# RMS norms of a two-block transformer kernel: 1/rms as exp(-0.5 ln(ms + eps)) on ScalarE, one table set preloaded

## The chip, the cores and the metric

The kernel runs as one launch on one core of a Trainium2 chip. The metric is the device time of that launch in microseconds. A core has TensorE (matmuls, writing PSUM), VectorE, ScalarE and GpSimd, each with an instruction queue of its own that it works off in order, and SyncE, which issues the transfers here. The engines wait for each other through semaphores: an instruction in a queue that waits holds up all that stands behind it.

## What is computed

The reference is a model of three layers on 256 tokens of width 1024: a gated short convolution with a SwiGLU feed-forward, a sliding-window attention with a SwiGLU feed-forward, and a hybrid layer (attention and a gated linear recurrence side by side) with a squared-ReLU feed-forward. There are eight norms over the width, and one of each head of 64 for q and k in the first attention:

```python
def rmsnorm(x, gain):
    xf = x.astype(jnp.float32)
    r = lax.rsqrt(jnp.mean(xf * xf, axis=-1, keepdims=True) + EPS)
    return (xf * r).astype(x.dtype) * gain

x = x + short_conv_mixer(rmsnorm(x, norm_mixer[0]), ...)      # mix0
x = x + swiglu_ffn(rmsnorm(x, norm_ffn[0]), ...)              # ffn0
x = x + swa_sink_attention(rmsnorm(x, norm_mixer[1]), ...)    # mix1
x = x + swiglu_ffn(rmsnorm(x, norm_ffn[1]), ...)              # ffn1
u = rms_norm(h, attn_pre_norm)                                # pre2
mix = hybrid_mixer(u, ...)
h = h + rms_norm(mix, attn_post_norm)                         # post2
u = rms_norm(h, mlp_pre_norm)                                 # mpre
m = jnp.square(jax.nn.relu(u @ w_mlp_up)) @ w_mlp_down
h = h + rms_norm(m, mlp_post_norm)                            # mpost
```

## The kernel before

Everything is held with the width on the partitions: x is 8 tiles of 128 features by 256 tokens. All weights stream from memory once, in pieces of 8 blocks of 128x128. Each piece is split into two numbers of lower precision: ScalarE rounds it (`round_weights`, L743, tile `whi`), VectorE forms the rest (`rest_weights`, L1139, tile `wlo`), and TensorE multiplies (`blocks`, L397 to L403) with the activations, which are split likewise into the halves of `xa`, `xb` or `hid`. Four piece slots and four accumulators (PSUM banks 0 to 3) go round. Every engine's program is an order written out by hand; `next_weights(n)` in the queues of ScalarE and VectorE prepares the piece that TensorE needs four pieces later. TensorE may start a piece when its `wlo` is there (`lo_ready`) and when the accumulator has been emptied (`emptied`).

The norm is not applied to x before the matmul. The gain is put on x, the matmul runs on that, and 1/rms (`rbc`, a tile of 128x256 that has each token's value on all partitions) is multiplied onto the result. Meanwhile ScalarE squares the tiles (`square`, L764), GpSimd adds the squares (`add_square`, L1592 and L1595, tile `ssum`), and TensorE sums over the partitions (`stat`, L411). Then it goes one of two ways.

- Plain norms (ffn0, mix1, ffn1, pre2): one matmul with a square of ones (L418) gives the sum on all partitions, ScalarE takes the square root over 128x256 (`rms`, L774), VectorE the reciprocal (L1171).
- The norms in `TURNED` (mix0, post2, mpre, mpost): four narrow matmuls (L422, L426) put the tokens' sums on the partitions, 128x2. They take the last squared tile directly from `sq`, without GpSimd's addition. ScalarE takes the root of 128x2 (L774), VectorE the reciprocal of 128x2 (L1169), two matmuls with the identity spread it over 128x256 (`spread`, L438), and ScalarE copies that to `rbc` (`copy_spread`, L779).

Square root, Exp, Ln, Silu, Sigmoid and Gelu of ScalarE come from sets of tables. Where an instruction needs a function that is not in the loaded set, the build puts an ACT_TABLE_LOAD in front of it. Two small square roots (L783, L1084) exist only to bring that load forward.

The stages and where the norms stand in the queues:

- mix0, `bx` body: ScalarE's `bx_step` (i = 0, p = 0) does the spill copy, the root, the rounding of the next body's first piece, then the copy to `rbc`. TensorE's order is `AS_LOADED`.
- ffn0, mix1, ffn1, pre2: `first_body` in the order `STAIR`, with the norm's sum between the pieces.
- `o`, `wo`: projections whose results are added to x (`residual_part`), the squares of the next norm beside them. `gated_down` does the same for `dn0` and `dn1`; beside `dn0` a few small Exp and Ln (`decay_constant`, L815 and L818).
- attention (328 to 380 us): the norms of k and q (L909, L916, L1344, L1350), then for each pair of heads scores, mask, maximum, Exp, division, transposition, values.
- post2: after the last piece of `out2`, TensorE runs three matmuls that only keep it busy (`keep_warm`, L432), the sum, the spread and four more of them. ScalarE has, in this order: square of the last tile, `rms`, `next_weights`, `copy_spread`. VectorE has copy, reciprocal, `next_weights` and then the residual chain (`post_scaled` L1531, `post_add` L1537, `norm_lo` L1177), tile by tile, which feeds both the squares of mpre and `mup`.
- mpre: TensorE's order is `ONE_BY_ONE`; ScalarE's `squared_up` (i = 0, p = 0) has `rms`, spill copy, rounding of the next body's first piece, copy to `rbc`; VectorE has reciprocal, rest of that piece, sum of the first accumulator (L1154), ReLU and scale (L1560).
- mpost: the tail. Sum, root, reciprocal, spread, copy, then VectorE and GpSimd scale eight tiles and add them to x, and SyncE stores.

Of the kernel before, what the change touches and what calls it, by code (L numbers as in the profile page):

```python
# [26 lines left out]
P = 128  # L27
# [82 lines left out]
def build(nc, bias_in_dram, x_in, stream, vecs_in, sinks_in, cons_in, out):  # L110
    with ExitStack() as ctx:
# [15 lines left out]
        rstd = sb("rstd", [P, TOK])  # L127
        rinv = sb("rinv", [P, 2])
# [32 lines left out]
        kstd = sb1("kstd", [P, 2, TOK])  # L161
# [5 lines left out]
        qstd = sb1("qstd", [P, 32])  # L167
# [23 lines left out]
        SUMS = 508  # L191
# [26 lines left out]
        rstd_ready = sem("rstd_ready")  # L218
        rinv_ready = sem("rinv_ready")
        spread_ready = sem("spread_ready")  # L220
# [14 lines left out]
        head_std = sem("head_std")  # L235
# [61 lines left out]
        TURNED = {NORM[name]: i for i, name in enumerate(("mix0", "post2", "mpre", "mpost"))}  # L297

        SQ0 = [sum(6 if m in TURNED else 7 for m in range(n)) for n in range(9)]

# [88 lines left out]
        def _(pe):  # L389
# [43 lines left out]

            def spread(norm):

                pe.wait_ge(rinv_ready, TURNED[norm] + 1)
                for tb in range(2):
                    ins = pe.matmul(bank[STAT][:, tb * P:(tb + 1) * P], rinv[:, tb:tb + 1].to_broadcast([P, P]),  # L438
                                    con("ident", P), start=True, stop=True)
                ins.then_inc(spread_ready, 1)  # L440

            def first_body(name, X, norm, split, split_at, order):
# [3 lines left out]
                for step in order:  # L446
                    if step == "norm":
                        if norm is not None:
                            stat(norm)
                        continue  # L450
                    if step == "spread":
                        if norm is not None:
                            spread(norm)
                        continue
# [18 lines left out]
                + [(KT - 3, KT, 0), (KT - 3, KT, 1), "norm", (KT - 3, KT, 2), "spread", (KT - 3, KT, 3)]  # L473
            AS_LOADED = [(0, 4, 0), (0, 4, 1), (4, 8, 0), (4, 8, 1), (0, 8, 2), "norm", (0, 4, 3), "spread", (4, 8, 3)]
# [204 lines left out]
            for r in range(4, AT["ba"]):  # L679
                n = R0 + r  # L680
                pe.wait_ge(lo_ready, n + 1)
                if AT["rg"] <= r < AT["v2"]:
# [4 lines left out]
                    if part == 0:  # L687
                        pe.wait_ge(rstd_ready, NORM["pre2"] + 1)
                        pe.wait_ge(taps, 3 * KT)
# [25 lines left out]
            spread(NORM["post2"])  # L715
# [14 lines left out]
            spread(NORM["mpost"])  # L730
# [3 lines left out]
        def _(act):  # L734
# [47 lines left out]
            act.wait_ge(warm_ready, 1)  # L782
            act.activation(scratch[:], pt1[:, 0, 0:1], ACT.Sqrt)  # L783
# [41 lines left out]
            def bx_step(i, p):  # L825
                spill_tile(4 * (B0["bx"] + i) + p, p)
                if i == 0 and p == 0:
                    rms(0)
                round_weights(B0["bx"] + i + 1, p)
                if i == 0 and p == 0:  # L830
                    copy_spread(0)
# [40 lines left out]
            def gated_down(name, gain, norm):  # L872
                for q in range(24):
# [16 lines left out]
            for t in range(12):  # L890
# [15 lines left out]
                if t == 6:  # L906
                    for j in range(2):
                        act.wait_ge(head_stat, j + 1)
                        act.activation(kstd[:, j, :], bank[ATT + j][:, 0:TOK], ACT.Sqrt, scale=1.0 / HD1, bias=EPS)\  # L909
                           .then_inc(head_std, 1)  # L910
# [5 lines left out]
            act.activation(qstd[:], bank[STAT][:, TOK:TOK + 32], ACT.Sqrt, scale=1.0 / HD1, bias=EPS)\  # L916
               .then_inc(head_std, 1)
# [156 lines left out]
            for t in range(8):  # L1074
# [25 lines left out]
            def squared_up(i):  # L1100
                for p in range(4):
# [4 lines left out]
                    if isinstance(i, int) and i == 0 and p == 0:  # L1106
                        copy_spread(NORM["mpre"])
# [19 lines left out]
            copy_spread(NORM["mpost"])  # L1127
# [3 lines left out]
        def _(dve):  # L1131
# [101 lines left out]
            def bx_step(i, p):  # L1233
# [101 lines left out]
            for t in range(12):  # L1335
# [5 lines left out]
                if t in (6, 7):  # L1341
                    j = t - 6
                    dve.wait_ge(head_std, j + 1)
                    dve.reciprocal(kinv[:, j, :], kstd[:, j, :]).then_inc(head_inv, 1)  # L1344
# [4 lines left out]
            dve.wait_ge(head_std, 3)  # L1349
            dve.reciprocal(rq[:], qstd[:]).then_inc(head_inv, 1)  # L1350
# [169 lines left out]
            for t in range(8):  # L1520
                dve.wait_ge(piece_done, 4 * B0["out2"] + t + 1)
                dve.tensor_copy(mix[:, t, :], acc(t)).then_inc(emptied, 1)
                if t == 7:
                    rms(NORM["post2"])
# [25 lines left out]
            def squared_up(i):  # L1550
                for p in range(4):
                    if isinstance(i, int) and i == 0 and p == 0:
                        rms(NORM["mpre"])
                        rest_weights(B0["mup"] + 1, 0)
                        dve.wait_ge(rbc_ready, NORM["mpre"] + 1)
# [20 lines left out]
            dve.wait_ge(rbc_ready, NORM["mpost"] + 1)  # L1576
# [8 lines left out]
        def _(pool):  # L1585
            def add_square(t, norm):
                if 1 <= t < (7 if norm in TURNED else 8):
# [277 lines left out]
```

## Time and profile before

| | us |
|---|---|
| median of 3 runs | 1043.62 (1041.79 to 1043.79) |
| the profiled execution's own time | 1043.98 |
| its span, first to last instruction | 1042.2 |
| TensorE busy (PE) | 1006.2, 97% of the span |
| VectorE busy (DVE) | 752.9, 72% |
| ScalarE busy (ACT) | 616.5, 59% |
| GpSimd busy (POOL) | 275.1, 26% |
| chain that ended last | PE 91%, DVE 4%, ACT 3% |
| mean granted TensorE clock | 0.99 of full speed |

In the profile PE is TensorE, PEld its weight loads, DVE VectorE, ACT ScalarE, POOL GpSimd. Times are in microseconds from the start of the span. L418 is line 418 of the kernel before. A matmul of plain f32 operands appears as two records of a weight load and a matmul each. The ends of matmuls are modelled. An engine's idle time in square brackets names the instruction that ended it.

### The profile page before, as it was taken

To read this page: it belongs to the slowest core of one execution; us is meant where nothing else is said; L and a number is where in the kernel's file an instruction comes from. 1 tells how busy PE (TensorE), PEld (TensorE's weight loads), DVE (VectorE), ACT (ScalarE), POOL (GpSimd) and SP (SyncE) were. 2 spreads that over 40 slices of the span, in tenths; PEclk is the share of its full clock that TensorE was granted. 3 is DMA by queue.
4 is the path that set the end of the run, shared out by engine and by line. 5 is a ranking of instruction groups with operands and counts; after the bars stand their busy time and mean duration, and the time that the engine had idled before them with its cause. 6 is when DMAs were issued, how large, how long until landed. Compare 5 with 4: busy or idle time off the path is not lost.

```text
span 1042.2 us, 20197 instructions
## 1 busy us (share of the span) xinstructions
PE 1006.2 (97%) x6888; PEld 924.8 (89%) x6888; DVE 752.9 (72%) x1154; ACT 616.5 (59%) x1093; POOL 275.1 (26%) x259
## 2 busy tenths in 40 slices
PE   8999999999997799999999999999999989999995
PEld 7899888889996598888898999999999978889995
DVE  6997877877667749877866787577866769775444
ACT  6555666656454757666645567867474558674441
POOL 2431232222100522232212236302031434441111
PEclk9999999999999899999999999999999999999997
DMA  8675555555553015555556554544444525545521
GB/s 311 231 298 183 182 196 186 181 177 192 192 198 125 2 52 194 201 199 186 170 178 203 191 188 177 167 158 162 156 160 162 198 95 202 183 179 202 187 97 41
DMA packets 26559, 180.93 MB, mean 174 GB/s; under 512 B 3072, under 2 KB 4224, under 8 KB 6144
## 3 DMA queue, kind: packets, MB, share of 16 engines
q1 hardware_dynamic: 26496, 180.07, 49.2%
q8 instruction: 42, 0.69, 0.3%
q14 instruction: 21, 0.17, 0.1%
HBM read 179.01 MB, written 1.05 MB: 173 GB/s over the span
## 4 chain that ended last, share of the span: by engine, by line
PE 91%; DVE 4%; ACT 3%; issue 1%; DMA 1%; SPq 0%; DVEq 0%; ACTq 0%
PE bank L397 34%; PE bank L403 29%; PE bank L399 13%; PE bank L401 12%; ACT pr L928 1%; DVE z L1531 1%; ACT whi L743 1%; DMA raw<-in_stream 1%; DVE x L1537 1%; DVE mx L1385 1%; DVE wlo L1139 0%; DVE xa L1177 0%; DVE mx L1378 0%; PE bank L641 0%; DVE sc L1365 0%
## 5 line engine op out<-in xcount | busy, mean ns | idle before, releaser
L1139 DVE TENSOR_TENSOR wlo<-raw,whi 128x1024 fp32r<-128x1024 f32 (+1 forms) x336 | 416.0, 1238 | 135.7 <-ACT whi L743 133.2
L743 ACT ACTIVATE whi<-raw 128x1024 fp32r<-128x1024 f32 (+2 forms) x336 | 351.4, 1046 | 177.2 <-PE bank L403 174.5
L403 PE MATMUL bank<-xa,wlo 128*128 128x256 f32 x1760 | 367.9, 280 | 0.0
L397 PE MATMUL bank<-xa,whi 128*128 128x512 f32 x1088 | 349.2, 397 | 4.4 <-DVE xa L1177 2.6
L403 PEld LDWEIGHTS bank<-xa,wlo 128*128 128x128 f32 x1760 | 312.8, 189 | 42.6
L399 PE MATMUL bank<-xa,whi 128*128 128x256 f32 x672 | 181.9, 289 | 0.0
L397 PEld LDWEIGHTS bank<-xa,whi 128*128 128x128 f32 x1088 | 170.2, 189 | 13.0 <-issue 2.4
L401 PE MATMUL bank<-xa,whi 128*128 128x256 f32 x672 | 177.6, 283 | 0.0
L754 ACT ACTIVATE spill<-bank 128x256 f32<-128x256 f32 x160 | 61.1, 382 | 141.4 <-PE bank L403 141.4
L397 PE MATMUL bank<-hid,whi 128*128 128x512 f32 x448 | 139.7, 393 | 0.0
L401 PEld LDWEIGHTS bank<-xa,whi 128*128 128x128 f32 x672 | 128.9, 192 | 0.3
L399 PEld LDWEIGHTS bank<-xa,whi 128*128 128x128 f32 x672 | 128.7, 191 | 0.3
L403 PEld LDWEIGHTS bank<-hid,wlo 128*128 128x128 f32 x608 | 108.7, 188 | 19.5
L403 PE MATMUL bank<-hid,wlo 128*128 128x256 f32 x608 | 121.1, 280 | 0.0
L1618 POOL TENSOR_TENSOR gate<-act,rbc 128x256 f32<-128x256 f32 x44 | 64.2, 1458 | 170.1 <-ACT act L865 164.1
L1154 DVE TENSOR_TENSOR z<-bank,spill 128x256 f32<-128x256 f32 x152 | 64.1, 421 | 45.7 <-ACT spill L754 44.2
L399 PE MATMUL bank<-xb,whi 128*128 128x256 f32 x288 | 79.4, 288 | 1.9 <-ACT rr L1049 1.5
L401 PE MATMUL bank<-xb,whi 128*128 128x256 f32 x288 | 78.5, 284 | 0.0
L1595 POOL TENSOR_TENSOR ssum<-ssum,sq 128x256 f32<-128x256 f32 x44 | 43.9, 998 | 109.3 <-ACT sq L764 108.7
L403 PE MATMUL bank<-xb,wlo 128*128 128x256 f32 x288 | 68.8, 284 | 0.0
L397 PEld LDWEIGHTS bank<-hid,whi 128*128 128x128 f32 x448 | 68.5, 188 | 0.0
L399 PEld LDWEIGHTS bank<-xb,whi 128*128 128x128 f32 x288 | 55.7, 193 | 3.1 <-issue 2.5
(206 smaller groups left out, 1127.5 us busy)
## 6 DMA issues: line engine op xcount, KB each, us to landing
raw<-in_stream SPq DMA_DIRECT2D x158, 1024.0 KB, 4.8
raw<-in_stream SPq DMA_DIRECT2D x8, 768.0 KB, 4.2
bias<-in_bias SPq DMA_DIRECT2D x1, 3072.0 KB, 12.8
raw<-in_stream SPq DMA_DIRECT2D x4, 512.0 KB, 7.9
x<-in_x SPq DMA_DIRECT2D x2, 512.0 KB, 6.2
out<-x SPq DMA_DIRECT2D x8, 128.0 KB, 2.0
cons<-in_cons SPq DMA_DIRECT2D x1, 640.0 KB, 9.3
vecs<-in_vecs SPq DMA_DIRECT2D x1, 77.0 KB, 2.1
```

What stands on the lines that cost most here:

```text
L397: pe.matmul(dst, whi[:, slot, at + i, :], X[:, k, :, :], start=first and i == 0, stop=False)
L399: pe.matmul(narrow, whi[:, slot, at + i, :], X[:, k, 0, :], start=first and i == 0, stop=False)
L401: pe.matmul(narrow, whi[:, slot, at + i, :], X[:, k, 1, :], start=False, stop=False)
L403: ins = pe.matmul(narrow, wlo[:, slot, at + i, :], X[:, k, 0, :], start=False, stop=last and i == len(tiles) - 1)
L743: act.activation(whi[:, p, 0:kts, :].rearrange("p k m -> p (k m)"), src, ACT.Copy)\
L754: act.activation(spill[:, slot, :], bank[slot][:, TOK:2 * TOK], ACT.Copy).then_inc(spilled, 1)
L928: act.activation(pr1[:, s, h, cols], sc1[:, s, h, cols], ACT.Exp, bias=nmx[:, s, j:j + 1], accum_out=den[:, s, j:j + 1])
L1139: dve.tensor_tensor(wlo[:, p, 0:kts, :].rearrange("p k m -> p (k m)"), src, whi[:, p, 0:kts, :].rearrange("p k m -> p (k m)").bitcast(F32) ...
L1154: dve.tensor_tensor(dst, acc(slot), spill[:, slot, :], ALU.add).then_inc(emptied, 1)
L1385: dve.tensor_tensor(mx[:, s, :], nmx[:, s, :], sinks[:, 4 * i:4 * i + 4], ALU.add).then_inc(negmax, 1)
L1595: pool.tensor_tensor(ssum[:], ssum[:], sq[:, t % 2, :], ALU.add).then_inc(sq_added, 1)
L1618: pool.tensor_tensor(gate[:, m, :], act1[:, m, :], rbc[:], ALU.mult).then_inc(gate_ready, 1)
```

## The change

- The norm's sum is a matmul with ones for all eight norms, on all partitions at once; for mix0, post2, mpre and mpost (`LATE`) a second one adds the last squared tile into the same accumulator. `spread` and the steps that called it go, and so does `copy_spread`.
- `rms` on ScalarE is Ln(sum / D + eps) into `lnms`, a wait for that, and Exp(-0.5 x) into `rbc`. VectorE's `rms` is only a wait for `rbc`; both kinds of reciprocal go. The norms of q and k are changed in the same way.
- The table set "natural_log_exp_and_others" is loaded explicitly at the start and ahead of `o`, `wo`, `dn0`, `dn1` and the sixth tile of `out2`. The two small square roots go.
- In `bx` and `mup` VectorE's wait for `rbc` stands behind the rest of the next piece, where the reciprocal stood ahead of it. TensorE's wait in `rg` is for `rbc` instead of `rstd`.

```diff
-        TURNED = {NORM[name]: i for i, name in enumerate(("mix0", "post2", "mpre", "mpost"))}
+        LATE = {NORM[name] for name in ("mix0", "post2", "mpre", "mpost")}
...
                 pe.wait_ge(sq_added, SQ0[norm + 1])
-                if norm not in TURNED:
-                    pe.matmul(bank[STAT][:, 0:TOK], con("ones", P), ssum[:], start=True, stop=True)\
-                      .then_inc(stat_ready, 1)
-                    return
-                for tb in range(2):
-                    pe.matmul(bank[STAT][:, SUMS + tb:SUMS + tb + 1], ssum[:, tb * P:(tb + 1) * P], con("ones", 1),
-                              start=True, stop=False)
-                    if tb == 0:
-                        pe.wait_ge(squared, 8 * norm + 8)
-                    ins = pe.matmul(bank[STAT][:, SUMS + tb:SUMS + tb + 1], sq[:, 1, tb * P:(tb + 1) * P],
-                                    con("ones", 1), start=False, stop=True)
+                ins = pe.matmul(bank[STAT][:, 0:TOK], con("ones", P), ssum[:], start=True, stop=norm not in LATE)
+                if norm in LATE:
+                    pe.wait_ge(squared, 8 * norm + 8)
+                    ins = pe.matmul(bank[STAT][:, 0:TOK], con("ones", P), sq[:, 1, :], start=False, stop=True)
                 ins.then_inc(stat_ready, 1)
...
-            def spread(norm):
-
-                pe.wait_ge(rinv_ready, TURNED[norm] + 1)
-                for tb in range(2):
-                    ins = pe.matmul(bank[STAT][:, tb * P:(tb + 1) * P], rinv[:, tb:tb + 1].to_broadcast([P, P]),
-                                    con("ident", P), start=True, stop=True)
-                ins.then_inc(spread_ready, 1)
...
             keep_warm(3)
             stat(NORM["post2"])
-            spread(NORM["post2"])
             keep_warm(4)
...
+            LOGS = "natural_log_exp_and_others"
+
             def rms(norm):
+
                 act.wait_ge(stat_ready, norm + 1)
-                n, at = (2, SUMS) if norm in TURNED else (TOK, 0)
-                act.activation(rstd[:, 0:n], bank[STAT][:, at:at + n], ACT.Sqrt, scale=1.0 / D, bias=EPS)\
-                   .then_inc(rstd_ready, 1)
-
-            def copy_spread(norm):
-                act.wait_ge(spread_ready, TURNED[norm] + 1)
-                act.activation(rbc[:], bank[STAT][:, 0:TOK], ACT.Copy).then_inc(rbc_ready, 1)
-
-
-            act.wait_ge(warm_ready, 1)
-            act.activation(scratch[:], pt1[:, 0, 0:1], ACT.Sqrt)
+                act.activation(lnms[:], bank[STAT][:, 0:TOK], ACT.Ln, scale=1.0 / D, bias=EPS).then_inc(ln_ready, 1)
+                act.wait_ge(ln_ready, norm + 1)
+                act.activation(rbc[:], lnms[:], ACT.Exp, scale=-0.5).then_inc(rbc_ready, 1)
+
+            act.preload_act_table_set(LOGS)
...
             def residual_part(name, gain, norm):
+                act.preload_act_table_set(LOGS)
...
             def gated_down(name, gain, norm):
+                act.preload_act_table_set(LOGS)
...
                 if t == 5:
-
-                    act.activation(scratch[:], con("ones", 1), ACT.Sqrt)
+                    act.preload_act_table_set(LOGS)
                 if t == 7:
                     next_weights(n)
-            copy_spread(NORM["post2"])
...
             def rms(norm):
-                dve.wait_ge(rstd_ready, norm + 1)
-                if norm in TURNED:
-                    dve.reciprocal(rinv[:], rstd[:, 0:2]).then_inc(rinv_ready, 1)
-                else:
-                    dve.reciprocal(rbc[:], rstd[:]).then_inc(rbc_ready, 1)
-                    dve.wait_ge(rbc_ready, norm + 1)
+                dve.wait_ge(rbc_ready, norm + 1)
...
                 if i == 0 and p == 0:
+                    rest_weights(B0["bx"] + i + 1, p)
                     rms(0)
-                    rest_weights(B0["bx"] + i + 1, p)
-                    dve.wait_ge(rbc_ready, 1)
```

## Rows read from the trace of the kernel before

**Rows 1.** Busy time by stage: stretch, its length, each engine's busy time (records), granted clock

```profile
core 0: us, PE busy (x) PEld busy (x) DVE busy (x) ACT busy (x) POOL busy (x), PEclk, DMA share, GB/s
17.00:327.00 310.00, 310.00 (x2050) 283.64 (x2048) 241.38 (x357) 180.49 (x294) 74.43 (x61) 1.00 0.57 202
...
382.00:650.00 268.00, 268.00 (x1798) 246.66 (x1798) 210.14 (x308) 167.90 (x276) 76.19 (x75) 1.00 0.54 189
```

**Rows 2.** Timeline at ffn0: start, duration, engine, line, operation, operands, [idle before <-releaser]

```profile
108.10 0.60 PE L418 MATMUL bank<-ssum,cons 128*128 128x256 f32 x2
108.73 0.38 ACT L774 ACTIVATE rstd<-bank 128x256 f32<-128x256 f32 x1 [3.52 <-PE bank L418]
109.15 1.75 DVE L1171 RECIPROCAL rbc<-rstd 128x256 f32<-128x256 f32 x1 [2.78 <-ACT rstd L774]
```

**Rows 3.** Timeline, ScalarE alone, in attention and behind it

```profile
348.77 0.37 ACT L948 ACTIVATE z<-bank 128x256 f32<-128x256 f32 x1
349.17 0.42 ACT L951 ACTIVATE xb<-z 128x256 fp32r<-128x256 f32 x1
...
380.37 0.49 ACT L768 ACTIVATE xa<-x,vecs 128x256 fp32r<-128x256 f32 x1
```

**Rows 4.** Timeline at mix0: the next body's first piece, on VectorE and TensorE

```profile
21.28 1.23 DVE L1139 TENSOR_TENSOR wlo<-raw,whi 128x1024 fp32r<-128x1024 f32 x1 [0.79 <-ACT whi L743]
...
23.29 0.62 PE L397 MATMUL bank<-xa,whi 128*128 128x512 f32 x2
```

**Rows 5.** Timeline, ScalarE at the head of attention

```profile
328.79 1.28 ACT L928 ACT_TABLE_LOAD   x1
332.27 0.40 ACT L928 ACTIVATE pr<-sc,nmx 128x128 f32<-128x128 f32 x1 [2.19 <-DVE mx L1385]
```

**Rows 6.** Timeline, ScalarE: a table load in dn0, and the start of wo's results

```profile
232.69 1.28 ACT L815 ACT_TABLE_LOAD   x1
233.98 0.21 ACT L815 ACTIVATE lamb<-lamb 128x8 f32<-128x8 f32 x1
...
379.40 1.06 ACT L743 ACTIVATE whi<-raw 128x1024 fp32r<-128x1024 f32 x1 [1.58 <-PE bank L403]
```

**Rows 7.** Timeline at post2, from the sum to mup's first matmul

```profile
839.95 0.28 PE L422 MATMUL bank<-cons,ssum 128*128 128x1 f32 x2
...
840.93 0.17 ACT L774 ACTIVATE rstd<-bank 128x2 f32<-128x2 f32 x1 [1.21 <-PE bank L426]
841.00 1.05 ACT L743 ACTIVATE whi<-raw 128x1024 fp32r<-128x1024 f32 x1
...
841.91 1.89 PE L432 MATMUL bank<-cons 128*128 128x256 f32 x8
842.08 1.22 DVE L1139 TENSOR_TENSOR wlo<-raw,whi 128x1024 fp32r<-128x1024 f32 x1 [0.78 <-ACT whi L743]
...
843.23 0.87 DVE L1531 SCALAR_TENSOR_TENSOR z<-q,vecs,rbc 128x256 f32<-128x256 f32 x2
...
845.83 0.47 PE L397 MATMUL bank<-xa,whi 128*128 128x512 f32 x1 [2.03 <-DVE xa L1177]
```

**Rows 8.** Timeline at mpre

```profile
858.36 1.06 ACT L743 ACTIVATE whi<-raw 128x1024 fp32r<-128x1024 f32 x1
...
861.07 0.74 PE L397 MATMUL bank<-xa,whi 128*128 128x512 f32 x2 [0.44 <-DVE z L1154]
```

**Rows 9.** Timeline at mpost, from the last square to the first scaled tile

```profile
1030.08 0.38 PE L426 MATMUL bank<-cons,sq 128*128 128x1 f32 x2 [0.85 <-ACT sq L764]
...
1032.74 1.91 DVE L1531 SCALAR_TENSOR_TENSOR z<-mres,vecs,rbc 128x256 f32<-128x256 f32 x2 [1.43 <-ACT rbc L779]
```

**Rows 10.** Busy time by stretch, columns as in rows 1: attention and post2

```profile
335.50:342.00 6.50, 4.98 (x26) 3.70 (x26) 5.64 (x16) 3.25 (x14) 3.08 (x4) 0.50 0.34 140
...
843.70:845.80 2.10, 0.10 (x1) 0.00 (x0) 2.06 (x7) 1.29 (x4) 0.00 (x0) 1.00 0.52 125
846.00:854.00 8.00, 8.00 (x41) 5.97 (x40) 8.00 (x16) 4.34 (x11) 4.17 (x6) 1.00 0.22 91
331.90:335.40 3.50, 0.00 (x0) 0.00 (x0) 3.46 (x11) 1.96 (x9) 0.04 (x1) 1.00 0.24 40
```

More of the change, by code:

```diff
@@ L126, in build @@
         ssum = sb("ssum", [P, TOK])
-        rstd = sb("rstd", [P, TOK])
-        rinv = sb("rinv", [P, 2])
+        lnms = sb("lnms", [P, TOK])
         rbc = sb("rbc", [P, TOK])
@@ L160, in build @@
         qkv = sb1("qkv", [P, 12, TOK])
-        kstd = sb1("kstd", [P, 2, TOK])
+        lnk = sb1("lnk", [P, 2, TOK])
         kinv = sb1("kinv", [P, 2, TOK])
@@ L166, in build @@
         pt1 = sb1("pt1", [P, 2, 3 * P])
-        qstd = sb1("qstd", [P, 32])
+        lnq = sb1("lnq", [P, 32])
         rq = sb1("rq", [P, 32])
@@ L234, in build @@
         head_stat = sem("head_stat")
-        head_std = sem("head_std")
+        head_ln = sem("head_ln")
         head_inv = sem("head_inv")
@@ L295, in build @@
         NORM = {"mix0": 0, "ffn0": 1, "mix1": 2, "ffn1": 3, "pre2": 4, "post2": 5, "mpre": 6, "mpost": 7}
-        TURNED = {NORM[name]: i for i, name in enumerate(("mix0", "post2", "mpre", "mpost"))}
-        SQ0 = [sum(6 if m in TURNED else 7 for m in range(n)) for n in range(9)]
+        LATE = {NORM[name] for name in ("mix0", "post2", "mpre", "mpost")}
+        SQ0 = [sum(6 if m in LATE else 7 for m in range(n)) for n in range(9)]
         R0 = 4 * B0["x2"]
@@ L449, in first_body @@
                             stat(norm)
[L450 to L453, printed above, removed]
                         continue
@@ L472, in _ @@
             ONE_BY_ONE = [(k, k + 1, p) for k in range(KT - 3) for p in range(4)] \
-                + [(KT - 3, KT, 0), (KT - 3, KT, 1), "norm", (KT - 3, KT, 2), "spread", (KT - 3, KT, 3)]
-            AS_LOADED = [(0, 4, 0), (0, 4, 1), (4, 8, 0), (4, 8, 1), (0, 8, 2), "norm", (0, 4, 3), "spread", (4, 8, 3)]
+                + [(KT - 3, KT, 0), (KT - 3, KT, 1), "norm", (KT - 3, KT, 2), (KT - 3, KT, 3)]
+            AS_LOADED = [(0, 4, 0), (0, 4, 1), (4, 8, 0), (4, 8, 1), (0, 8, 2), "norm", (0, 8, 3)]
             IN_ORDER = [(0, 8, p) for p in range(4)]
@@ L687, in _ @@
                     if part == 0:
-                        pe.wait_ge(rstd_ready, NORM["pre2"] + 1)
+                        pe.wait_ge(rbc_ready, NORM["pre2"] + 1)
                         pe.wait_ge(taps, 3 * KT)
@@ L729, in _ @@
             stat(NORM["mpost"])
-            spread(NORM["mpost"])
         @block.scalar
@@ L829, in bx_step @@
                 round_weights(B0["bx"] + i + 1, p)
-                if i == 0 and p == 0:
-                    copy_spread(0)
             for i in range(4):
@@ L908, in _ @@
                         act.wait_ge(head_stat, j + 1)
-                        act.activation(kstd[:, j, :], bank[ATT + j][:, 0:TOK], ACT.Sqrt, scale=1.0 / HD1, bias=EPS)\
-                           .then_inc(head_std, 1)
+                        act.activation(lnk[:, j, :], bank[ATT + j][:, 0:TOK], ACT.Ln, scale=1.0 / HD1, bias=EPS)\
+                           .then_inc(head_ln, 1)
+                        act.wait_ge(head_ln, j + 1)
+                        act.activation(kinv[:, j, :], lnk[:, j, :], ACT.Exp, scale=-0.5).then_inc(head_inv, 1)
                 if t == 7:
@@ L915, in _ @@
             act.wait_ge(head_stat, 10)
-            act.activation(qstd[:], bank[STAT][:, TOK:TOK + 32], ACT.Sqrt, scale=1.0 / HD1, bias=EPS)\
-               .then_inc(head_std, 1)
+            act.activation(lnq[:], bank[STAT][:, TOK:TOK + 32], ACT.Ln, scale=1.0 / HD1, bias=EPS).then_inc(head_ln, 1)
+            act.wait_ge(head_ln, 3)
+            act.activation(rq[:], lnq[:], ACT.Exp, scale=-0.5).then_inc(head_inv, 1)
             def exps1(i):
@@ L1105, in squared_up @@
                     round_weights(B0["mup"] + i + 1, p)
-                    if isinstance(i, int) and i == 0 and p == 0:
-                        copy_spread(NORM["mpre"])
                     if p > 0 or not isinstance(i, int):
@@ L1126, in _ @@
             rms(NORM["mpost"])
-            copy_spread(NORM["mpost"])
         @block.vector
@@ L1522, in _ @@
                 dve.tensor_copy(mix[:, t, :], acc(t)).then_inc(emptied, 1)
-                if t == 7:
-                    rms(NORM["post2"])
                 next_weights(4 * B0["out2"] + t)
@@ L1552, in squared_up @@
                     if isinstance(i, int) and i == 0 and p == 0:
+                        rest_weights(B0["mup"] + 1, 0)
                         rms(NORM["mpre"])
-                        rest_weights(B0["mup"] + 1, 0)
-                        dve.wait_ge(rbc_ready, NORM["mpre"] + 1)
                     if not isinstance(i, int):
@@ L1575, in _ @@
             rms(NORM["mpost"])
-            dve.wait_ge(rbc_ready, NORM["mpost"] + 1)
             post_scaled(mres, "mpost", 0, final, 0)
@@ L1586, in add_square @@
             def add_square(t, norm):
-                if 1 <= t < (7 if norm in TURNED else 8):
+                if 1 <= t < (7 if norm in LATE else 8):
                     pool.wait_ge(squared, 8 * norm + t + 1)
```

9 lines of the change are left out of this document (1 added, 8 removed).

## The prediction

> **What bounds the kernel now.** I first looked at TensorE's idle time, stage by stage, because a faster norm can only pay where somebody on the path waits for it. In the table by stage TensorE is busy for every microsecond from 17 to 327 us and from 382 to 650 us [rows 1]. Five of the eight norms lie in those two stretches: mix0 (about 20 us), ffn0 (108), mix1, ffn1 and pre2 (about 293, 399 and 584). So there the work behind the norm is hidden, and only a change of TensorE's own work, or a new stall, can move the end. Then I read the timeline around the three others, post2 (840 us), mpre (858) and mpost (1030), where TensorE does stand idle. Last I looked at attention (328 to 380 us), which is bound by latency, and whether the change touches its chain.
>
> **Prices of the operations.** A ones matmul of a full row (128x256 f32) is two records in 0.60 us, and ScalarE starts 0.03 us behind it; the square root over 128x256 takes 0.38 us and VectorE's reciprocal 1.75 us [rows 2]. No Ln and no such Exp of 128x256 is in the profile of before. The nearest rows are ScalarE's operations of that shape: 0.37 us out of PSUM, 0.42 us out of SBUF, with 0.03 us between the first and a second that waits for it on the same engine [rows 3]. I take Ln 0.38, gap 0.03, Exp 0.42; the dearest of these rows, 0.49 us for one with a vector as scale, is the upper bound of each, the cheapest, 0.37, the lower one. An unrelated instruction behind the Exp overlaps its end by about 0.1 us (a square root at 840.93 lasts 0.17, the next starts at 841.00) [rows 7].
>
> **The four plain norms (ffn0, mix1, ffn1, pre2).** The reciprocal (1.75) goes and an Exp (0.42) comes, so rbc is ready about 1.3 us earlier; in mix1, ffn1 and pre2 a table load of 1.28 us goes too. At ffn0 the reciprocal ends at 110.90 [rows 2] and TensorE does not notice it. It never waits in these stages, and its own work is the same one matmul. I cost them at nothing: the cover is TensorE's own queue of weight pieces, which were rounded ahead; if that cover were gone each would give 1.3 us.
>
> **mix0.** TensorE loses the four spread records. VectorE's wlo of the next body's first piece starts at 21.28, behind ScalarE's whi, and TensorE reaches that piece at 23.29 [rows 4]. Now Ln and Exp stand ahead of whi in ScalarE's queue where a narrow square root stood (0.17, and whi 0.07 behind its start, as at post2) [rows 7]. The last record of two wide matmuls ends about 0.07 us later than that of the eight narrow ones, and 0.38 + 0.03 + 0.42 - 0.10 = 0.73 takes the place of that 0.07, so whi and wlo move by 0.07 + 0.73 - 0.07 = 0.73. wlo then ends at 21.28 + 0.73 + 1.23 = 23.24, and TensorE starts at 23.30. It would be there already at about 22.9 because of the missing spread, so the gain of 0.4 is eaten by a new stall on wlo: sum 0.0, between -0.1 and +0.2.
>
> **Attention and the q and k norms.** Two reciprocals of 1.75 leave VectorE between 312 and 318 us and ScalarE gets two Exps, all under a busy TensorE. The q norm's Exp over 32 columns takes the place of a reciprocal over 32, a few tenths either way before the first mask (-0.2 to +0.2, taken as 0). The load of 1.28 us at 328.79 goes, but ScalarE then stood idle for 2.19 us before the first softmax Exp, so it was hidden [rows 5]. Nothing.
>
> **The preloads.** Two loads in dn0 go and one comes; o and wo each get one that was not there, dn1 too, and out2's takes the place of the old one. A load costs 1.28 us of ScalarE's time, and the instruction behind it starts at once (232.69 + 1.28 = 233.97, next at 233.98) [rows 6]. The tight place is wo: ScalarE waits 1.58 us for TensorE, from 377.82 on, before its next whi at 379.40 [rows 6], and the wlo behind that whi is what TensorE needs next. 1.28 fits in 1.58 with 0.3 to spare: nothing. The Trainium skill ("ScalarE: Activation LUTs", What ACT_TABLE_LOAD costs) says otherwise: 1283 ns for the load and a drain of about 1380 ns, 2.66 us per switch. By it the preload would end at 380.5 and push the chain by 1.1 us, an estimate from that section. The trace agrees with the 1283 ns; [rows 6] show no drain.
>
> **post2, where the path runs over ScalarE's queue.** Here I followed the chain backwards from TensorE's first matmul of mup (845.83): it waits for the residual chain on VectorE, which starts at 843.23. That start does not wait for rbc, which was ready before; it waits for VectorE's wlo (842.08 to 843.30), which waits for ScalarE's whi (841.00), which is queued directly behind the norm's narrow square root [rows 7]. In the changed kernel the whi is queued behind Ln and Exp: same sum as at mix0, +0.73 us. What was saved, the reciprocal of two columns, the four spread records and the copy, was hidden behind whi. The whole residual chain follows: +0.73, between +0.6 and +0.95.
>
> **mpre.** The same again. Spill and whi (858.36) stand behind the narrow root, then wlo and the sum on VectorE, for which TensorE waits 0.44 us at 861.07 [rows 8]. Ln and Exp push spill and whi by 0.73; the wait absorbs nothing, since TensorE is already early, and its saved spread only makes it wait longer. +0.73, between +0.6 and +0.95.
>
> **mpost, the tail.** Nothing is queued behind it, so the full latency counts. Before: the last square's matmul starts at 1030.08, the first scaled tile at 1032.74 [rows 9]. After: 1030.08 + 0.12 (weights) + 0.60 + 0.03 = 1030.83 for Ln if the matmul is as in rows 2, 1030.71 if its weights are already counted in the start; then 0.38 + 0.03 + 0.42 + 0.04. First tile at 1031.58 to 1031.70: -1.1 us, between -0.9 and -1.2.
>
> **Sum.** 0.0 + 0.73 + 0.73 - 1.1 = +0.36, say +0.4. The profiled execution (span 1042.2, its own time 1043.98) lies 0.36 above the median of the three runs, 1043.62. So 1044.3 for it, 1044.0 for the median.
>
> **The rivals.** *The clock at post2.* Before, TensorE runs four warming matmuls behind the spread (841.91 on), and stands idle for 2.03 us until 845.83; the granted clock stays at 1.00 (2.4 GHz) [rows 7, 10]. Now there is no wait for a spread: the warming ones follow the sum at once and end at 839.95 + 0.85 + 1.7 = 842.5, and the first matmul comes at 846.56. That is 4.1 us of idling. In attention TensorE did nothing from 331.9 to 335.4, and the clock stood at 0.50 (1.2 GHz) from there to 342 [rows 10]. 4.1 us of idling is nearer to the case that lost the clock. Price: if it lasts as long as there, 6.5 us, half of it, 3.3 us, is lost at most. But between 846 and 854 TensorE has 41 records, 20 steps of 512 and 256 columns, 6.6 us of streaming at 2.4 GHz in 8 us, so some 1.4 us are free, and the first part of a slow stretch lies in the idling. 0 to 2.0 us, about 0.8: 1044.8. *The set is not kept (slower).* If the preloaded set does not count for Ln or Exp, each pair brings two loads: at 1.28 x 2 on mix0, post2, mpre and mpost that is +10 us, 1054. It decides as soon as one load stands between Ln and Exp. For it speaks that Exp and Ln were in two loads before in dn0 (Exp's at 232.69) [rows 6]; against it that each load in the profile stands only where the function changes. *A load holds ScalarE longer than its record.* If it held it twice the record, 2.57 us, the whi at wo would slip by 2.57 - 1.58 = 1.0: 1045.0. The row at 233.98, which starts right behind the record, speaks against it. The Trainium skill's drain, above, is this case. *The saved VectorE time pays (faster).* If the plain norms' 1.3 us each counted in two or three places after all, -3: 1041; TensorE's full busy time speaks against it.
>
> **How the numbers follow.** Forecast (clock cost below 0.3) 0.50; clock 0.34; set not kept 0.03; load longer than its record 0.03; VectorE time pays 0.04; the rest, drift between runs (the three runs span 2.0 us, 1041.79 to 1043.79), 0.06, half each way. A measurement of this kernel tells about 0.2% from no change, which is 2.1 us. Slower by more: set not kept, a fifth of the clock case, a little of the rest: 0.12. Faster by more: 0.05. Range: from 1042.3 (drift downward, all bounds low) to 1045.9 (the clock's 2.0 with the forecast).
>
> **What would show it.** ACT's whi behind post2's and mpre's norms starts 0.7 us later relative to the stat matmul, wlo and the residual chain with it; the tail from the last square to the first scaled tile shrinks from 2.66 to about 1.55; TensorE's clock row around 845 to 852 says whether the rival came; ACT_TABLE_LOAD counts say whether the set was kept. I am wrong if TensorE shows new waits in the plain norms' stages, or if the load at wo delays whi.

## The result, and the profile after

| | before | changed |
|---|---|---|
| median, range | 1043.38 (1041.79 to 1045.5, 8 runs) | 1046.62 (1044.92 to 1047.05, 8 runs) |
| ratio, 95% interval | | 1.0028 (1.0017 to 1.0039) |
| profiled execution: time, span | 1043.98, 1042.2 | 1047.05, 1045.3 |
| granted TensorE clock | 0.990 | 0.988 |

The change makes the kernel 0.28% slower; the forecast was 1044.0 us with a range up to 1045.9. Ratios here and below leave out the executions far above the rest of their kernel, one of C (1235.19 us, at a granted clock of 0.75) and one of the kernel before that ran beside K (1993.49). The page of the changed kernel (share of the span, instructions) shows the engines almost as before, VectorE 13 us lighter, and TensorE 0.9 us busier although it has 32 matmuls fewer:

```profile
span 1045.3 us, 20125 instructions
PE 1007.1 (96%) x6856; PEld 925.2 (89%) x6856; DVE 740.0 (71%) x1143; ACT 617.1 (59%) x1096; POOL 274.8 (26%) x259
```

**The prices.** Groups of ScalarE's instructions by line (busy us, mean ns | idle before):

```profile
L753 ACT ACTIVATE rbc<-lnms 128x256 f32<-128x256 f32 x8 | 3.3, 417 | 0.3
L751 ACT ACTIVATE lnms<-bank 128x256 f32<-128x256 f32 x8 | 3.1, 384 | 19.3 <-PE bank L413 12.5 <-PE bank L416 6.8
L816 ACT ACT_TABLE_LOAD x2 | 2.6, 1283 | 0.0
```

Ln takes 0.384 us and Exp 0.417; 0.38 and 0.42 had been taken. No load stands between them: the set is kept. The load at wo is hidden, as said from [rows 6]: it starts at 377.82, and the whi behind it at 379.39, still behind a wait for TensorE:

```profile
377.82 1.28 ACT L816 ACT_TABLE_LOAD   x1
379.39 1.06 ACT L718 ACTIVATE whi<-raw 128x1024 fp32r<-128x1024 f32 x1 [0.29 <-PE bank L399]
```

This load brings in the set that is already there, since no other load stands between it and dn0's at 227.79. The two at dn0 and dn1 (227.79 and 518.76) do change sets, from that of Silu, and the whi behind each starts 1.29 us after the load.

**post2.** Timeline of the changed kernel, to be read against [rows 7]:

```profile
841.16 0.59 PE L416 MATMUL bank<-sq,cons 128*128 128x256 f32 x2
...
841.59 1.89 PE L421 MATMUL bank<-cons 128*128 128x256 f32 x8
841.79 0.38 ACT L751 ACTIVATE lnms<-bank 128x256 f32<-128x256 f32 x1 [1.28 <-PE bank L416]
842.21 0.42 ACT L753 ACTIVATE rbc<-lnms 128x256 f32<-128x256 f32 x1
842.53 1.04 ACT L718 ACTIVATE whi<-raw 128x1024 fp32r<-128x1024 f32 x1
843.60 1.22 DVE L1109 TENSOR_TENSOR wlo<-raw,whi 128x1024 fp32r<-128x1024 f32 x1 [3.54 <-ACT whi L718]
844.75 0.87 DVE L1489 SCALAR_TENSOR_TENSOR z<-q,vecs,rbc 128x256 f32<-128x256 f32 x2
...
847.35 0.77 PE L393 MATMUL bank<-xa,whi 128*128 128x512 f32 x1 [3.87 <-DVE xa L1142]
```

This is the predicted chain: whi starts 0.74 behind Ln, and wlo, the residual chain and mup's first matmul follow it. The first matmul lasts 0.77 in place of 0.47 (ends are modelled), and TensorE idled 3.87 us before it: the clock rival is there too. In the busy time by stretch the granted clock is the column PEclk; 0.50 is 1.2 GHz, 1.00 is 2.4:

```profile
core 0: us, PE busy (x) PEld busy (x) DVE busy (x) ACT busy (x) POOL busy (x), PEclk, DMA share, GB/s
839.50:844.70 5.20, 3.98 (x19) 3.17 (x18) 1.52 (x2) 2.16 (x4) 0.23 (x1) 1.00 0.20 85
847.00:853.50 6.50, 6.15 (x19) 5.30 (x20) 6.50 (x13) 3.32 (x9) 3.26 (x4) 0.50 0.32 135
```

**mpre and mpost.** At mpre TensorE's wait grows from 0.44 [rows 8] to 1.62. At mpost the last square's matmul starts at 1034.21 and Ln 0.73 behind it; 0.63 or 0.75 had been summed. The first scaled tile starts 1.60 behind that matmul, where it was 2.66 [rows 9]:

```profile
864.05 0.74 PE L393 MATMUL bank<-xa,whi 128*128 128x512 f32 x2 [1.62 <-DVE z L1124]
...
1034.21 0.70 PE L416 MATMUL bank<-sq,cons 128*128 128x256 f32 x2 [0.53 <-ACT sq L739]
1034.94 0.38 ACT L751 ACTIVATE lnms<-bank 128x256 f32<-128x256 f32 x1 [0.25 <-PE bank L416]
1035.36 0.42 ACT L753 ACTIVATE rbc<-lnms 128x256 f32<-128x256 f32 x1
1035.81 1.92 DVE L1489 SCALAR_TENSOR_TENSOR z<-mres,vecs,rbc 128x256 f32<-128x256 f32 x2 [2.10 <-ACT rbc L753]
```

At mix0 the new stall that was forecast is there too: TensorE waits 0.44 us for wlo before the next body's first matmul (22.81).

```profile
22.81 0.72 PE L393 MATMUL bank<-xa,whi 128*128 128x512 f32 x2 [0.44 <-DVE wlo L1109]
```

**Where the rest is.** I cut the span at matmuls that both kernels have, counted in TensorE's order, and took the time between the starts at the cuts. This table, for all kernels below too, is worked out from those starts ("post2": last matmul of out2 to first of mup; "mup, first": from there to the first of the second body, so mpre is in it; "tail": from the last matmul to the end). The cuts lie not quite at the stages' borders: dn0 and dn1 are cut 33 matmuls behind their start and 24 ahead of their end, mdn 67 behind its start, and what is cut off counts in the row ahead or behind. The letters are the experiments below:

| stage, us | before | changed | A fill | B before+32 | C weights first | D warm 9 | E fill at hid | F before turned |
|---|---|---|---|---|---|---|---|---|
| mix0 | 6.27 | 6.36 | 6.37 | 6.26 | 5.81 | 6.36 | 6.37 | 6.25 |
| bx to up0 | 208.56 | 208.72 | 208.67 | 208.48 | 208.59 | 208.66 | 208.65 | 208.58 |
| dn0 | 53.09 | **53.74** | 53.09 | 53.50 | 53.09 | 53.09 | 53.09 | 53.09 |
| qkv, attention | 96.84 | 96.49 | 96.54 | 96.91 | 96.53 | 96.44 | 96.53 | 98.13 |
| wo to up1 | 140.66 | 140.72 | 140.66 | 140.56 | 140.66 | 140.66 | 140.65 | 140.67 |
| dn1 | 53.09 | **53.74** | 53.09 | 53.50 | 53.09 | 53.09 | 53.09 | 53.09 |
| x2 to out2 | 263.01 | 263.09 | 263.00 | 263.04 | 263.02 | 263.00 | 263.02 | 263.01 |
| post2 | 7.29 | 8.04 | 8.03 | 7.29 | 5.95 | 8.03 | 8.03 | 6.60 |
| mup, first | 15.24 | 16.70 | 16.26 | 15.21 | 14.16 | 15.97 | 15.94 | 14.68 |
| mup, rest | 89.91 | 90.04 | 89.89 | 89.96 | 89.80 | 89.89 | 89.88 | 89.90 |
| mdn | 77.86 | **78.87** | 77.86 | 78.43 | 77.86 | 77.86 | 77.86 | 77.86 |
| tail | 13.33 | 12.31 | 12.32 | 13.14 | 12.32 | 12.33 | 12.32 | 13.15 |

dn0, dn1 and mdn together take 2.31 us longer within these cuts. From the first matmul of each to its last it is 2.6 us: 61.77 to 62.51 in dn0 and in dn1, 89.62 to 90.75 in mdn. Nothing of a norm runs in the middle of them. There TensorE never waits; its matmuls follow each other more slowly, in all of the stage. These three, and no others, stream `hid` as the moving operand. The diff touches `hid` in one way only: `rinv` stood ahead of it in SBUF, the memory that holds the tiles. The tiles are laid one behind the other in slots of 32 bytes, so without `rinv` (8 bytes, one slot) every tile behind it starts 32 bytes lower, `hid` at byte 139744 of the partition in place of 139776. The same group of TensorE's instructions before and after (ns min/median/max, first and last start; mdn's narrow matmuls):

```profile
L399 PE MATMUL bank<-hid,whi x64: 274/281/287, 956.0 to 1028.5; 128*128 128x256 f32 x64
```

```profile
L395 PE MATMUL bank<-hid,whi x64: 278/280/281, 959.2 to 1032.6; 128*128 128x256 f32 x64
```

72.5 us from the first to the last became 73.4. The duration of one is modelled and shows nothing; the starts do.

### The profile page after: what moved, and what is told of

It reads as the page before. It is cut to its first block, busy times and chain, and to the rows that moved or that the text cites. A ratio compares the mean times of both kernels' runs of the same rounds, so it can differ in the third digit from the quotient of the medians.

```text
span 1045.3 us, 20125 instructions
## 1 busy us (share of the span) xinstructions
PE 1007.1 (96%) x6856; PEld 925.2 (89%) x6856; DVE 740.0 (71%) x1143; ACT 617.1 (59%) x1096; POOL 274.8 (26%) x259
## 4 chain that ended last, share of the span: by engine, by line
PE 92%; DVE 3%; ACT 3%; issue 1%; DMA 1%; SPq 0%; DVEq 0%; ACTq 0%
PE bank L393 34%; PE bank L399 30%; PE bank L395 13%; PE bank L397 12%; ACT pr L903 1%; ACT whi L718 1%; DVE wlo L1109 1%; DVE mx L1345 1%; DMA raw<-in_stream 1%; DVE z L1489 1%; DVE mx L1338 0%; PE bank L618 0%; PE bank L413 0%; DVE x L1495 0%; DVE sc L1325 0%
```

## The experiments

**A, the address.** The changed kernel with an unused tile in `rinv`'s slot:

```
+        sb("fill", [P, 2])
         rbc = sb("rbc", [P, TOK])
```

> The changed kernel with one unused tile of 2 numbers per partition in front of rbc, where rinv lay, so that every tile behind it, hid among them, has the address of the kernel before (hid at byte 139776 of a partition; 139744 in the changed kernel). Theory A (addresses): in the stages that stream hid (dn0, dn1, mdn) TensorE's slow drift of +0.6, +0.7 and +1.1 us against before disappears; 2.4 us faster than the changed kernel, ratio to before about 1.0005 (+0.5 us: post2 +0.7, mpre +0.7, the low clock +0.7, tail -1.1, with run to run drift). Rival B (the drift comes from what the new norm does, not from where the tiles lie): the drift stays and the ratio is 1.0028 as for the changed kernel.

Measured: 1044.02 (1042.41 to 1045.55, 12 runs), ratio to before 1.0000 (0.9990 to 1.0009). The three stages are back at 53.09, 53.09 and 77.86. The address is the cause of 2.3 us within the cuts and of 2.6 in the whole stages, which is also what lies between the medians (1046.62 and 1044.02). The kernel before had a median of 1043.74 beside A to D, 1043.36 beside E and F, and 1043.37 beside K.

**B, the kernel before, moved the other way** (8 floats, one slot, ahead of `rbc`: `hid` at 139808):

> The kernel before with one unused tile of 8 numbers per partition in front of rbc: nothing else is changed, hid moves from byte 139776 to 139808, which is again 32 bytes off a multiple of 64. Theory A: the drift of the changed kernel appears in the kernel before, +2.4 us, ratio 1.0023, all of it in dn0, dn1 and mdn. Rival B: same time as before, ratio within 1.0005.

Measured: 1045.1 (1043.25 to 1046.34, 11 runs), ratio 1.0013 (1.0005 to 1.0022). +1.39 us in the three stages (0.41, 0.41, 0.57), and no other stage longer by more than 0.1: the address acts without the change. The size was missed: 2.4 us had been expected, so 32 bytes up do not cost what 32 bytes down do.

**E, hid alone.** The two floats moved from ahead of `rbc` to just ahead of `hid`:

> The two unused floats now stand only just ahead of hid: every tile from rbc to rden keeps the byte address that it has in the changed kernel, and hid and mres alone go back to where they were before (hid at byte 139776). Theory (the address of hid, which TensorE streams in dn0, dn1 and mdn, is what costs): the stages last 53.1, 53.1 and 77.9 us as before, and the ratio to before is 1.000 (0.999 to 1.001), as with the tile ahead of rbc. Rival (the address of one of the tiles from rbc on, such as the gains or the constants, costs): the stages stay at 53.7, 53.7 and 78.9, and the ratio stays at 1.002 to 1.003.

Measured: 1042.89 (1042.32 to 1044.22, 11 runs), ratio 0.9997 (0.9988 to 1.0006), all stages as in A but for mup's first body (see D). It is `hid`, not the vectors or constants. (The tiles of the other stages that share `hid`'s place, such as `qkv` and `u`, move with it; dn0 and dn1 use none of them.)

**C, the order of ScalarE's queue.** A, and at mix0, post2 and mpre the next piece's whi goes ahead of Ln and Exp (post2 shown; at the others `round_weights` goes ahead of `rms`, at mpre together with the spill copy):

```
-                if t == 7:
-                    rms(NORM["post2"])
...
                 if t == 7:
                     next_weights(n)
+                    rms(NORM["post2"])
```

> As e1_fill, and at mix0, post2 and mpre ScalarE rounds the next piece of weights ahead of Ln and Exp instead of behind them. My reading of the path (C): what the change loses at post2 and mpre is the 0.73 us by which whi, wlo and what waits for them are pushed. With the order turned round the rbc is ready about 841.9 on the clock of the trace of before, wlo is earlier, so the residual chain starts 1.2 us earlier than before; at mpre TensorE's wait of 0.44 and the spread go (-0.8); at mix0 -0.4; the tail -1.1 as in the changed kernel; and TensorE idles some 2 us less at post2, so the clock is kept. Sum -3.5 us against before, ratio 0.9966, 1039.9. Rival D (Ln and Exp themselves, or the removed spread, are the loss, wherever they stand): within 0.5 us of e1_fill.

Measured: median 1039.42 (five runs from 1037.94 to 1039.52, and the one named above), ratio 0.9955 (0.9942 to 0.9967), faster than both kernels. Against A: post2 -2.08, mup's first body -2.10, mix0 -0.56 us, 4.7 together; the medians are 4.6 apart. Against before: -1.34, -1.08, -0.46 and -1.01 in the tail, beside -1.2, -0.8, -0.4 and -1.1 expected. The timeline of C at post2 shows whi in the time in which ScalarE used to wait for the sum, and rbc ready before wlo ends:

```profile
838.75 1.04 ACT L719 ACTIVATE whi<-raw 128x1024 fp32r<-128x1024 f32 x1
840.12 0.38 ACT L752 ACTIVATE lnms<-bank 128x256 f32<-128x256 f32 x1 [0.34 <-PE bank L417]
840.54 0.42 ACT L754 ACTIVATE rbc<-lnms 128x256 f32<-128x256 f32 x1
...
840.99 0.88 DVE L1489 SCALAR_TENSOR_TENSOR z<-q,vecs,rbc 128x256 f32<-128x256 f32 x2
```

**F, the same order in the kernel before** (whi ahead of the square root at the same three places; VectorE's order kept, its small reciprocal ahead of wlo):

> The kernel before with nothing but ScalarE's order turned at mix0, post2 and mpre: the next weight piece's whi goes ahead of the norm's square root. Ln and Exp, the wide ones matmul and the preloads are not in it. Theory (the gain of the run with the weights first is the order's, not that of Ln and Exp): post2 gets about 0.8 us shorter, because VectorE's wlo no longer waits for whi but only stands behind the small reciprocal (841.22 in place of 842.08), mpre about 0.8 to 1.1, mix0 0 to 0.4, together -1.6 to -2.3: ratio 0.998. Rival (only a norm that needs no VectorE lets the weights go first; here the root, the reciprocal and the spread now come later and rbc becomes the late one): within 0.5 us of before, ratio 1.000.

Measured: 1042.05 (1040.53 to 1043.71, 11 runs), ratio 0.9991 (0.9982 to 1.0000). post2 -0.69, mup's first body -0.56, mix0 -0.02: 1.3 us by the stages, less than the 1.6 to 2.3 of the theory and more than the 0.5 of the rival. The interval of the whole kernel does not exclude the rival. The timeline at post2 says why it ends there. The root, the reciprocal, the spread and the copy come one after the other until 843.40. VectorE's wlo stands behind the reciprocal, and so behind the norm's sum, and ends at 843.36. The residual chain starts behind both:

```profile
842.05 0.17 DVE L1166 RECIPROCAL rinv<-rstd 128x2 f32<-128x2 f32 x1 [1.86 <-ACT rstd L774]
842.14 1.22 DVE L1136 TENSOR_TENSOR wlo<-raw,whi 128x1024 fp32r<-128x1024 f32 x1
842.27 0.71 PE L438 MATMUL bank<-cons,rinv 128*128 128x128 f32 x4 [0.46 <-DVE rinv L1166]
...
843.02 0.38 ACT L779 ACTIVATE rbc<-bank 128x256 f32<-128x256 f32 x1 [1.00 <-PE bank L438]
843.44 0.88 DVE L1528 SCALAR_TENSOR_TENSOR z<-q,vecs,rbc 128x256 f32<-128x256 f32 x2
```

So the order alone is worth 1.3 us to the old norm, and Ln with Exp nothing without it (A); both together 4.3 against before (C). The new norm pays here only once the weights stand ahead of it on ScalarE, and in C VectorE has no step of the norm ahead of its wlo either.

**D, the clock at post2.** A, with nine warming matmuls in place of four behind post2's sum:

```
-            keep_warm(4)
+            keep_warm(9)
```

> As e1_fill, but nine matmuls instead of four keep TensorE busy behind post2's sum, 2.1 us more, which leaves about 2 us of idling, as in the kernel before. Theory (clock): the low clock behind post2 does not come, and against e1_fill 0.7 us are gained, which the trace of the changed kernel shows between mup's first matmul and mpre's sum (+0.73 against before); ratio to before about 1.0000. Rival: TensorE's slack of 1.4 us hid the low clock, and it is the same as e1_fill, within 0.2 us. If the additional warming delayed something, mup's first matmul would come later than in e1_fill.

Measured: 1043.85 (1042.45 to 1046.04, 11 runs), ratio 1.0000 (0.9991 to 1.0009). The clock is kept at post2, and mup's first body takes 15.97 in place of 16.26 in A and 16.70 in the changed kernel. Rows of 846 to 854 us of A and of D:

```profile
846.00:854.00 8.00, 7.72 (x31) 6.67 (x32) 8.00 (x16) 4.52 (x12) 4.04 (x5) 0.66 0.27 112
```

```profile
846.00:854.00 8.00, 6.29 (x33) 4.78 (x32) 7.96 (x17) 4.20 (x10) 3.28 (x4) 1.00 0.36 131
```

The granted clock of this stretch and the length of mup's first body go together only in part: 0.57 with 16.70 (changed), 0.66 with 16.26 (A), but 0.79 with 15.94 (E), as short as D at 1.00. So by the profiles the low clock costs between 0 and 0.7 us, since TensorE has some slack there. The medians of A and D are 0.17 apart, less than their spread and far from the 0.7 expected; the rival, that the slack hides it, is not excluded for the whole kernel. The same stretch stood at 0.79 in B, whose post2 is that of before to 0.01 us: the clock is lost there in some executions and not in others.

**What of the address counts.** Six kernels, of which the last is also a candidate. Those with one run are read by their stages, which repeat to a few hundredths of a us between kernels where nothing differs. First `hid` 64 bytes above its old place (24 floats ahead of `rbc`):

> The changed kernel with 24 unused floats ahead of rbc: hid at byte 139840, a multiple of 64 but not of 128. If the moving operand only has to start at a multiple of 64 bytes, dn0, dn1 and mdn last 53.1, 53.1 and 77.9 us. If it has to be 128 or 512, they last 53.5 to 53.7, 53.5 to 53.7 and 78.4 to 78.9, as with 139808 or 139744.

Measured: 1040.38 in one run; dn0 and dn1 52.20, mdn 76.53, which is 3.1 us *less* than before. Both expectations fail: the old address was no optimum. mdn's narrow matmuls need 71.2 us:

```profile
L396 PE MATMUL bank<-hid,whi x64: 275/277/277, 954.7 to 1025.9; 128*128 128x256 f32 x64
```

Then the moving operand of the other stages, and the stationary one. In G `xa` and `xb` start 32 bytes further (8 floats ahead of `xa`, 24 behind `xb`), in H `whi` and `wlo` do (8 ahead of `whi`, 24 behind `wlo`):

> The changed kernel with hid where it was before, and xa and xb, the moving operands of the other stages, 32 bytes further (8 unused floats ahead of xa, 24 behind xb, so that all later tiles move by 128 bytes and hid stays on a multiple of 128). If the cost belongs to any moving operand that starts 32 bytes off a multiple of 64, the stages that stream xa (208.6, 140.7 and 263.0 us) get about 1% longer, +5 to +8 us in all, and dn0, dn1 and mdn stay at 53.1, 53.1 and 77.9. If it is something of hid or of its neighbours alone, every stage stays.

> The same for the stationary operand: whi and wlo 32 bytes further (8 unused floats ahead of whi, 24 behind wlo), xa, xb and hid on multiples of 64. If only the moving operand matters, no stage changes (53.1, 53.1, 77.9, 208.6, 263.0). If any operand of TensorE matters, all stages get about 1% longer, +8 to +11 us in all.

G: 1033.12 in one run, the opposite of what was expected: the stages of `xa` and `xb` get *shorter*. H: 1048.59 in one run, 4.5 us longer than the kernel before beside it, where 8 to 11 had been expected if any operand mattered; the stages do not all get longer by the same share. So it is not a matter of multiples of 64 bytes, and the stationary operand's address counts as well. The next idea was that only the distance between the two counts. Kernel I is A with 8 floats ahead of the first tile: all tiles move by 32 bytes, and each distance is kept. In J only what lies from `xa` on moves, by 96:

> The changed kernel with the two unused floats (hid at 139776) and 8 more ahead of the very first tile: every tile, moving and stationary operands alike, 32 bytes further, all distances between them kept. If what counts is where the moving operand lies relative to the stationary one (or to any other tile), no stage changes: 208.6, 53.1, 140.7, 53.1, 263.0 and 77.9 us. If the address itself counts, the stages show what each operand showed when it was shifted alone by 32: dn0 and dn1 53.5, mdn 78.4 for hid, and a change of 2 us or more in the stages that stream xa and xb (206.5 and 257.4 us where xa and xb alone were shifted).

> The changed kernel with xa, xb, hid and all tiles behind xa 96 bytes further than in the kernel before; whi and wlo stay. If the distance from the weights counts, modulo 128 or 256, this is the look with the weights shifted by 32 and the rest by 128 again: to dn0 210.7, x2 to out2 263.2, dn0 53.3, mdn 78.3 us. If the addresses themselves count, the stages of xa and xb show values not seen yet.

| stage, us | A | G: xa +32, hid +128 | H: weights +32, xa, hid +128 | I: all +32 | J: xa, hid +96 | K: C, xa, hid +64 |
|---|---|---|---|---|---|---|
| xa, hid from the weights | 0, 0 | +32, +128 | +96, +96 | 0, 0 | +96, +96 | +64, +64 |
| bx to up0 | 208.67 | 206.48 | 210.66 | 208.67 | 209.25 | 204.58 |
| dn0 (dn1 the same) | 53.09 | 53.18 | 53.33 | 53.09 | 53.33 | 52.20 |
| wo to up1 | 140.66 | 139.75 | 142.17 | 140.66 | 142.17 | 139.28 |
| x2 to out2 | 263.00 | 257.37 | 263.16 | 263.02 | 263.13 | 258.78 |
| mup, rest | 89.89 | 89.51 | 91.07 | 89.89 | 91.07 | 89.01 |
| mdn | 77.86 | 78.07 | 78.25 | 77.86 | 78.25 | 76.53 |

I took 1042.40 us and J 1046.81, in one run each. The first row is how much further `xa` and `hid` lie from the weights than in the kernel before. Kernel I moves every address and changes none of these stages by more than 0.02 us (attention alone, where the clock differed, is 1.5 shorter). H and J have other addresses and the same distances, and agree within 0.03 us in all stages but the first (210.66 and 209.25). Most of that difference lies in up0, 124.71 us in H and 123.63 in J, while up1, the same matmuls on the same tiles, takes 124.7 in both: something besides the addresses goes into the pace, and what it is stays open. In the rest, the distance in bytes between where the moving and the stationary operand lie is what counts, and not the addresses themselves. It isn't quite periodic in 128: 0 and +128 give 53.09 and 53.18, -32 and +96 give 53.74 and 53.33.

**K, both gains.** C with `xa`, `xb`, `hid` and all behind `xa` 64 bytes further:

```
         wlo = sb("wlo", [P, 4, 8, P], F32R)
         x = sb("x", [P, KT, TOK])
+        sb("off_xa", [P, 16])
         xa = sb("xa", [P, KT, 2, TOK], F32R)
```

> The kernel with the weights first, and in addition xa, xb, hid and all tiles behind xa 64 bytes further. hid: dn0 and dn1 52.2, mdn 76.5 us, as in the look with hid at 64 (-3.1 us together). xa and xb were seen at 0 and at 32 bytes (-8.7 us together at 32), not at 64. If they go like hid (best at 64, -1.7% of the stages), the stages that stream them lose some 10 us, and the kernel lands at 1026 to 1028 us, ratio 0.984; if only hid gains, at 1036, ratio 0.993; if 64 is bad for xa, at 1040 or above.

Measured: 1025.19 (1023.55 to 1025.19, 5 runs), ratio 0.9822 (0.9807 to 0.9836): 1.8% faster than before, of which 0.45% is C (new norm and order) and the rest (1039.42 to 1025.19) the 64 bytes; 1026 to 1028 had been expected if `xa` and `xb` went like `hid`. It is the best version found. Its page: TensorE has the 6856 matmuls of the changed kernel and is busy for 21 us less.

```profile
span 1021.8 us, 20125 instructions
PE 986.0 (96%) x6856; PEld 908.4 (89%) x6856; DVE 741.8 (73%) x1143; ACT 617.3 (60%) x1096; POOL 275.8 (27%) x259
```

## Why the prediction was wrong, by its own steps

- **The stages that TensorE fills, the step that failed.** The prediction said that there "only a change of TensorE's own work, or a new stall, can move the end", and gave dn0, dn1 and mdn no term in the sum. There is a third way: the same matmuls at another pace. Removing `rinv` moved `hid`, and dn0, dn1 and mdn got 2.6 us longer, 2.3 of it within the cuts (A, B and E show it). With it the sum of +0.4 becomes +3.0, and 1043.6 + 3.0 = 1046.6 beside the 1046.62 measured. That it fits to the tenth is luck in part: in the two profiles the clock's 0.7 at post2 and the attention's -0.35 are not in this sum. No row of before could price the pace; the diff shows that `hid` moves, so the question could have been asked.
- **Plain norms**: nothing forecast, and right. TensorE has no new waits there, and the cuts with ffn0, ffn1 and pre2 changed by 0.16, 0.06 and 0.08, which holds some of the matmuls on `hid` too. mix1 lies in the cut with the attention, below.
- **mix0**: 0.0 forecast, +0.09 measured, with the forecast stall on wlo (0.44).
- **post2 and mpre**: +0.73 each forecast; +0.75 (8.04 against 7.29), and 15.97 against 15.24 = +0.73 where the clock was kept (D). The reason is right too: with the weights ahead of Ln and Exp (C) the loss is gone and more.
- **mpost**: -1.1 forecast, -1.02 measured (13.33 to 12.31).
- **Attention**: 0 forecast. In the profiles it is 0.3 to 0.4 shorter in the changed kernel, A, C, D and E, from one Exp in the middle of the attention loop on. The q norm isn't it: the kernel before and A reach the first softmax Exp 0.03 us apart. What makes it was not followed. The stage also varies with the clock, from 95.04 (I, granted clock 1.00 from 345 to 381 us) to 98.13 (F, 0.91) with no change to attention in either, so a single profile can't settle tenths here.
- **Preloads**: hidden, as said. The rival that a load holds ScalarE longer than its record is dead: the whi behind the one at wo is not late, and behind the loads that change sets the next instruction starts at 1.29 us. The drain that the Trainium skill ("ScalarE: Activation LUTs", What ACT_TABLE_LOAD costs) adds to the 1283 ns is not seen in this trace: the whi behind the load at 518.76 starts at 520.05, and by the 2.66 us that the section gives it would start at 521.4, an estimate.
- **Clock rival**: it came, after 3.87 us of idling where 4.1 had been worked out, and cost 0 to 0.7 us by the profile, beside the 0.8 that it was given. Alone it would have stayed within the range.
- **What was luck**: without the address (A) the medians are 0.28 us above before, beside the +0.36 of the sum. But A's profile has +0.3 from the clock and -0.3 from the attention, which the sum has not, and they cancel.
- **Set not kept**: no load between Ln and Exp; dead.

## What to carry to other kernels

A change that adds or removes a small tile moves everything behind it: compare the pace of the matmuls in stages that the change doesn't touch, and put a filler in the slot before judging the idea. Where a kernel is bound by TensorE, try its moving operands 32 and 64 bytes further from the weights; here that was worth 14 us, three times the reordering. And work whose inputs are already there (the next weights) goes ahead of a wait on its queue, not behind it, above all when the path runs over that work, as over whi and wlo here.

## What the hardware showed that was not expected

- The time between matmuls depends on the distance between the moving and the stationary operand in SBUF: dn0 lasts 52.20, 53.09, 53.33, 53.50 or 53.74 us at +64, 0, +96, +32 and -32 bytes. x2 to out2, which streams `xa` and `xb` in matmuls of 256 columns only, takes 263.0, 257.4, 258.8 and 263.1 at 0, +32, +64 and +96. In up1 `xa` is streamed in matmuls of 512 and of 256 columns, and there +64 is best, as for `hid`: 123.2, 122.6, 122.1 and 124.7 from its first matmul to that of dn1. So the best distance differs from stage to stage, for the same tile too. The Trainium skill ("TensorE: Matmul & The Clock Gate", Step-by-step: what each phase is for) says that TensorE has two independent read ports of SBUF and that loading the next weights does not take bandwidth from the running matmul. From it one would expect no effect of the distance; I against G, H and J shows that there is one. No run here shows by what mechanism.
- The clock falls to 1.2 GHz at post2 in some executions of the same work and not in others. Before it fell TensorE had idled for 3.87 us in the changed kernel. In D, whose warming matmuls run on longer, and in C it idles for 1.7 to 1.8 us, and the clock stayed at 2.4 GHz; in B it idles for 2.03 us as before, and the clock fell in part (0.79).
